# Joining two tap sums on GpSimd in a depthwise convolution of 31 taps

## The reference, cut to what matters

```
u = h @ w_in + b_in;  a, g = split(u);  u = a * sigmoid(g)
u = depthwise_conv(pad_left(u, 30), w_dw)  + b_dw      # 31 taps per channel
u = silu(layer_norm(u));  u = u @ w_out + b_out
```

## Time and profile before

| what | us |
|---|---|
| median of 3 runs (2560.78 to 2561.13) | 2560.98 |
| span of the profiled execution | 2562.9 |
| TensorE busy | 2541.8 (99%) |
| VectorE busy | 1751.1 (68%) |
| ScalarE busy | 1278.0 (50%) |
| GpSimd busy | 470.5 (18%) |

### The profile page before, as it was taken

How to read it: one execution, slowest core, us unless ns; L and a number is a source line. 1 busy time by engine, 2 the same in 40 slices (tenths; PEclk the granted TensorE clock), 3 DMA queues, 4 the chain that set the end, 5 groups by cost and what they waited for, 6 DMA issues and landing times. The chain is left out here.

```text
span 2562.9 us, 43939 instructions
## 1 busy us (share of the span) xinstructions
PE 2541.8 (99%) x15061; PEld 2254.1 (88%) x15061; DVE 1751.1 (68%) x2126; ACT 1278.0 (50%) x1615; POOL 470.5 (18%) x302
## 2 busy tenths in 40 slices
PE   9999999999999999999999999999999999999999
PEld 8888888888888888888888899988788888888888
DVE  7578875587765665665667889985766556665666
ACT  5456555554544444444445555455644444444445
POOL 5034410001100000000011378862400000000003
PEclk9999999999999999999999999999999999999999
DMA  7655565665666566666655655536465656665564
GB/s 230 187 170 175 164 181 182 198 194 179 188 188 188 182 196 188 188 190 187 190 188 178 193 165 161 164 111 193 148 190 187 189 173 195 194 189 183 188 187 142
DMA packets 497441, 465.33 MB, mean 182 GB/s; under 512 B 14505, under 2 KB 494243, under 8 KB 497315
## 3 DMA queue, kind: packets, MB, share of 16 engines
q1 hardware_dynamic: 496816, 463.92, 58.9%
q10 hardware_dynamic: 546, 0.38, 0.1%
HBM read 462.15 MB, written 2.10 MB: 181 GB/s over the span
## 5 line engine op out<-in xcount | busy, mean ns | idle before, releaser
L1340 DVE TENSOR_TENSOR wlo<-stage,whi 128x1024 fp32r<-128x1024 f32 x811 | 1027.9, 1281 | 663.8 <-ACT whi L797 657.4
L412 PE MATMUL gp<-A,whi 128*128 128x512 f32 x4224 | 1406.3, 394 | 5.7 <-DVE A L1792 2.9
L797 ACT ACTIVATE whi<-stage 128x1024 fp32r<-128x1024 f32 x876 | 917.3, 1057 | 951.9 <-PE gp L415 740.7
L415 PE MATMUL gp<-A,wlo 128*128 128x256 f32 x3456 | 970.9, 281 | 0.0
L412 PEld LDWEIGHTS gp<-A,whi 128*128 128x128 f32 x4224 | 788.3, 188 | 180.8 <-issue 6.9
L412 PE MATMUL gp<-B,whi 128*128 128x512 f32 x2216 | 772.2, 393 | 0.7 <-issue 0.7
L415 PEld LDWEIGHTS gp<-A,wlo 128*128 128x128 f32 x3456 | 652.9, 189 | 0.0
L415 PE MATMUL gp<-B,wlo 128*128 128x256 f32 x2216 | 620.1, 280 | 0.0
L412 PEld LDWEIGHTS gp<-B,whi 128*128 128x128 f32 x2216 | 415.0, 187 | 95.5 <-issue 1.1
L415 PEld LDWEIGHTS gp<-B,wlo 128*128 128x128 f32 x2216 | 418.4, 189 | 0.0
L1981 POOL TENSOR_TENSOR sq<-r 128x512 f32 (+1 forms) x32 | 43.0, 1343 | 806.1 <-DVE r L1606 756.0
(11 more groups left out here) (310 smaller groups left out, 1470.8 us busy)
## 6 DMA issues: line engine op xcount, KB each, us to landing
stage<-in_w_in SPq DMA_DIRECT2D x160, 512.0 KB, 4.4
stage<-in_w_up SPq DMA_DIRECT2D x128, 512.0 KB, 3.9
stage<-in_w_down SPq DMA_DIRECT2D x128, 512.0 KB, 3.7
stage<-in_ffn_w_gate SPq DMA_DIRECT2D x88, 512.0 KB, 4.3
stage<-in_ffn_w_up SPq DMA_DIRECT2D x88, 512.0 KB, 4.4
stage<-in_ffn_w_down SPq DMA_DIRECT2D x88, 512.0 KB, 4.4
stage<-in_conv_w_in SPq DMA_DIRECT2D x64, 512.0 KB, 4.1
stage<-in_w_o SPq DMA_DIRECT2D x32, 512.0 KB, 4.5
```

What stands on the lines that cost most here:

```text
L412: nc.tensor.matmul(bank.rearrange("p (a t) -> p a t", a=2), hi, both_parts(M, kt), start=first, stop=False)
L415: done = nc.tensor.matmul(bank[:, T:2 * T], lo, M[:, kt, 0:T], start=False, stop=last)
L797: nc.scalar.activation(whi[:, slot, :], stage[:, slot, :], ACT.Copy).then_inc(hi_ready, 1)
L1340: nc.vector.tensor_tensor(wlo[:, slot, :], stage[:, slot, :], whi[:, slot, :].bitcast(F32), ALU.subtract).then_inc(lo_ready, 1)
```

## The change

TensorE does one tap of tiles 0 to 14 in place of two (`PE_TAPS` 1, so `DVE_END` is 30), and VectorE does taps up to 29. The last odd tap is now 29 and still writes `V[:, i]`. For tiles 0 to 13 the last even tap (28) no longer writes PSUM but a tile in SBUF, `even_sum[:, i % 2]`; from tile 2 on it first waits until the join of tile i-2 is done. VectorE's `both_sums` is left only for tiles 14 and 15. GpSimd's new `add_sums(i-1)` stands in pass i behind `take_lo` of unit 1, waits for all of VectorE's taps of tile i-1, adds the two sums and signals `v_ready`.

```
-PE_TAPS = 2
+PE_TAPS = 1
+POOL_TILES = 14
+        even_sum = area(diag_at + PE_LAST * P, 2, T)
...
-                        nc.vector.scalar_tensor_tensor(V[:, i, :] if t == last_odd else o, x, w, o,
-                                                       ALU.mult, ALU.add).then_inc(tap_done, 1)
+                        dst = V[:, i, :] if t == last_odd else o
+                        if t == last_odd - 1 and i < POOL_TILES:
+                            if i >= 2:
+                                dve.wait_ge(v_ready, i - 1)
+                            dst = even_sum[:, i % 2, :]
+                        nc.vector.scalar_tensor_tensor(dst, x, w, o, ALU.mult, ALU.add).then_inc(tap_done, 1)
...
-                    both_sums(i - 1, xp[:, 2 + (i - 1) % 2, :], DVE_END, v_ready)
+                    if i - 1 >= POOL_TILES:
+                        dve.wait_ge(v_ready, POOL_TILES)
+                        both_sums(i - 1, xp[:, 2 + (i - 1) % 2, :], DVE_END, v_ready)
...
+            def add_sums(i):
+                pool.wait_ge(tap_done, taps_before(i + 1))
+                nc.gpsimd.tensor_tensor(V[:, i, :], V[:, i, :], even_sum[:, i % 2, :], ALU.add).then_inc(v_ready, 1)
...
                     take_lo(n0 + RING + 4 * i + u, u)
+                    if u == 1 and 1 <= i <= POOL_TILES:
+                        add_sums(i - 1)
```

## The result

The changed kernel takes 2649.54 us (median of 5 runs, 2646.8 to 2649.79) against 2560.98. The ratio is 1.0338, 95% interval 1.0328 to 1.0349: +86.6 us (84.0 to 89.4). The two medians lie 88.6 us apart, within this interval. The forecast was 2653.7, +92.7.

What follows compares the result with a forecast made beforehand. TensorE, busy 99%, was taken as the bound; the join's wait would make it stand in each conv2 tile. Loop and extra tap +59.1, clock +33.6: +92.7 us on 2560.98, 2653.7; range 2613 to 2667.

Steps and rivals of the forecast that it cites:

- The place of the wait: GpSimd's join behind unit 1 waits 9.8 us for VectorE's last tap, holding low halves of units 2 and 3.
- the loop: End of tile i, VectorE's remaining taps, join, unit 2's low half, TensorE's units 2 and 3: 16.8 us against 12.90.
- The turn: One round of the conv2 loop between scaled_pair starts: 16.8 us against 12.90, TensorE standing 4.3 us per tile.
- The clock: TensorE's clock falls in each of 14 stands and recovers in units 2 and 3: 14 x 2.4 = 33.6 us.
- the two recoveries of the earlier trace: TensorE's clock returned 3.5 or 6.0 us after dense work; at half rate 1.75 or 3.0 us lost.
- the middle of the two: Loss per clock fall on TensorE taken as 2.4 us, between 1.75 and 3.0.
- 2 us from dense work to the fall: TensorE's clock falls 2 us after dense work, so a 4.3 us stand brings a fall each time.
- Rival A: Same conv2 loop, but clock holds or seldom falls; slot 3 loads add some tenths per tile: 2620 to 2624, 20%.
- Rival B: GpSimd's join is hidden and VectorE sets the conv2 pace: 4.0 us gained, 2557, 4%.
- Rival C: Additions only fill GpSimd; passes with two more additions need 12.9 us, gain and loss cancel: 2561, 3%.
- tile 14's extra tap: VectorE's last conv2 pass has the extra tap and still the sum, delaying the stage's end: +0.4 us.

Runs made afterwards that it cites:

- the deferred join: Changed kernel with GpSimd's join of tile i-2, instead of tile i-1, behind unit 1 of pass i: ratio to before 0.9983, -4.4 us.
- the wait alone: Changed kernel with joins back on VectorE and only GpSimd's wait for the last tap in each join's place: ratio to before 1.0276, +70.7 us.
- the kernel with the clock held up: Changed kernel with 17 unused 128-column matmuls behind TensorE's tap of each tile, in front of unit 2: ratio to before 1.0262, +67.1 us.
- the kernel with the old shares of taps: Changed kernel with joins in place, but TensorE keeping two taps and VectorE 28: ratio to before 1.0303, +77.6 us.

## Why the prediction was right

**The place of the wait.** It said GpSimd comes to the join 9.8 us ahead of the last tap and holds units 2 and 3. The profile has 14 waits, 106.1 us in all, and TensorE stands 14 times. The waits were shorter than forecast: 5.5 to 9.2 us where it had 7 to 10, five of them under 7. The 9.8 was read from a trace without the loop. In the loop the wait is what GpSimd's own work leaves of the turn (four low halves of 9.4 us, the join, and up to two additions of 1.3), and the five follow turns with one or two such additions. That the mechanism stands is shown by the deferred join (no wait, no loss) and the wait alone (82% of the loss).

**The turn.** 16.8 was forecast from the rows of before, and 16.6 measured where the clock is set aside. The 0.2 us is in the handovers, which I added to rows that already reach over them: the join takes 0.69 to the next instruction, not 0.73, and 2.40 bring TensorE's start where I had 2.41 + 0.08. Over 13 turns this is 3 us.

**The clock.** It fell in all 14 stands, as forecast, and with the two recoveries of the earlier trace rows. The size was off: I took half of the time at the lower clock as lost, and it is 0.45 (0.227 and 0.125 us per matmul), so 1.5 and 2.6 us where I had 1.75 and 3.0. That the middle of the two would serve held: the short recovery is about as frequent as the long. Mean loss 2.1 us per turn, not 2.4. With the turn this makes 18.7 in place of 19.2. `scaled_pair(15)` started at 1771.99; the sum had 1779.4 (1745.8 + 14 x 2.4), and 84.9 us later than before, not 92.3. The premise that led to the falls, 2 us from dense work to the fall, did not hold: in the changed kernel the clock fell 2.9 to 4.9 us after TensorE stopped, and in six of the 14 turns only up to 0.4 us after it had started again. So the falls were less safe than the sum made them. In the main the trace agrees with the page "TensorE: Matmul & The Clock Gate" of the Trainium skill, section "HAM oscillation — how this bites in real kernels": a loop that waits between bursts starts each at the low clock. Here eight of 14 started at it and six fell to it within 0.4 us; the mean clock was 0.86 from 1502 to 1773.

**The loads.** Rival A's "some tenths per tile" was right in its place: 0.46 us per turn in the kernel with the clock held up.

**The other side.** Rival B asked for a GpSimd that is never late, and gave 2557 for it; the deferred join is that kernel, and is 4.4 us under before. Rival C (12.9 us passes from GpSimd's load) did not come up: in the deferred kernel the 13 turns from `scaled_pair(1)` to `scaled_pair(14)` are 12.40 or 12.41 us, those with two more additions too.

**What stayed.** VectorE's busy time stayed (1751.1 and 1752.5), and the tail kept its length (875.8 us from `scaled_pair(15)` to the end before, 875.7 after). The 0.4 us that I gave tile 14's extra tap are not to be seen.

## What to carry to other kernels

A free engine is not a free place in its queue. Before work is moved to an engine that feeds another one in order, find the time at which its operand is ready and the time at which the engine gets there; if it gets there first, count what lies behind it and when that is needed. Here the cure was to put the work a pass later: the same change cost 86.6 us with its 14 additions in one place and gained 4.4 with them in the next.

## What the runs showed of the hardware

A stand of 3.0 to 6.3 us in every turn (58.1 us in 14) was enough for TensorE's clock to fall to 0.50 each time, just before the restart or up to 0.4 us after it, and it came back 3.4 or 5.8 us after the restart in the turns looked at. Matmuls without use in the stand kept it at 1.00, and the kernel with them was 19 us faster than the one without.

The length of a stand alone did not decide it. In the kernel with the wait alone a stand of 2.3 us (restart at 1605.68) had no fall. In the kernel with the old shares of taps one of 2.2 us had (restart at 1608.97), and with the join behind unit 2 one of 1.8.

The stand's cost went with the length of the turn. In the kernel with the wait alone nine of 13 turns had the length of the short recovery, in the changed kernel six, so that taking away 0.7 us of path gave 1.2 us per turn (18.68 to 17.50). I had expected one loss for all; that the length is the cause was not tried by itself.

At the lower clock a matmul of 272 columns came every 0.227 us, at the full one every 0.125: 1.8 times, not twice.
